# Attention masks: from identity matmuls on TensorE to the pass for the maxima on VectorE

## The reference

```python
logits = jnp.where(key_pos[None, :] <= q_pos[:, None], logits, -jnp.inf)   # layer 1
p = jax.nn.softmax(logits, axis=-1)

s = jnp.where(mask, s, NEG_INF)                                             # layer 2
m = jnp.max(s, axis=-1, keepdims=True)
e = jnp.where(mask, jnp.exp(s - m), 0.0)
```

## Time and profile before

| | us |
|---|---|
| median of 3 runs | 1828.26 (1828.24 to 1828.29) |
| span of the profiled execution | 1826.9 |
| TensorE busy | 1812.1 |
| VectorE busy | 1039.6 |
| ScalarE busy | 657.3 |
| GpSimd busy | 36.1 |

### The profile page before, as it was taken

How to read it: one execution, slowest core, us unless ns; L and a number is a source line. 1 busy time by engine, 2 the same in 40 slices (tenths; PEclk the granted TensorE clock), 3 DMA queues, 4 the chain that set the end, 5 groups by cost and what they waited for, 6 DMA issues and landing times.

```text
span 1826.9 us, 25140 instructions
## 1 busy us (share of the span) xinstructions
PE 1812.1 (99%) x9052; PEld 1510.2 (83%) x9052; DVE 1039.6 (57%) x1764; ACT 657.3 (36%) x1273; POOL 36.1 (2%) x58
## 2 busy tenths in 40 slices
PE   9999999999999999999999999999999999999998
PEld 7888888888888888878878887888888888888887
DVE  7544434434433788853358865666667666775334
ACT  6433323222223544432236343334333333343222
POOL 0000000000000000000002000000000000000001
PEclk9999999999999999999999999999999999999999
DMA  6322222222232333232238364212212222224332
GB/s 234 120 98 76 81 94 91 81 83 82 86 107 71 137 104 126 93 117 96 92 100 229 112 211 137 70 46 68 71 46 81 81 69 80 69 69 138 116 115 104
DMA packets 54179, 186.37 MB, mean 102 GB/s; under 512 B 6688, under 2 KB 7584, under 8 KB 53600
## 3 DMA queue, kind: packets, MB, share of 16 engines
q1 hardware_dynamic: 49536, 170.78, 28.2%
q0 software_dynamic: 4576, 14.68, 2.9%
HBM read 177.05 MB, written 8.39 MB: 102 GB/s over the span
## 4 chain that ended last, share of the span: by engine, by line
PE 93%; DVE 4%; DVEq 1%; ACT 1%; issue 0%; DMA 0%; SPq 0%; ACTq 0%
PE strip L430 23%; PE strip L432 23%; PE strip L431 23%; PE scores L430 3%; PE scores L431 3%; PE scores L432 3%; PE outputs L432 2%; PE outputs L431 2%; PE outputs L430 2%; PE scores L485 1%; PE scores L537 1%; PE scores L545 1%; PE scores L958 1%; PE scores L541 1%; PE scores L917 1%; PE scores L986 1%
## 5 line engine op out<-in xcount | busy, mean ns | idle before, releaser
L430 PE MATMUL strip<-xh,wh 128*128 128x512 f32 (+1 forms) x1896 | 745.7, 393 | 2.3 <-DVE xl L1968 1.3
L432 PE MATMUL strip<-xh,wl 128*128 128x512 f32 (+1 forms) x1896 | 735.5, 388 | 0.0
L431 PE MATMUL strip<-xl,wh 128*128 128x512 f32 (+1 forms) x1896 | 735.0, 388 | 0.0
L1567 DVE TENSOR_TENSOR wl<-raw,wh 128x1024 fp32r<-128x1024 f32 (+3 forms) x306 | 354.9, 1177 | 140.9 <-ACT wh L1074 140.1
L430 PEld LDWEIGHTS strip<-xh,wh 128*128 128x128 f32 x1896 | 356.3, 188 | 74.9 <-DVE xl L1968 2.6
L432 PEld LDWEIGHTS strip<-xh,wl 128*128 128x128 f32 x1896 | 356.0, 188 | 74.0
L431 PEld LDWEIGHTS strip<-xl,wh 128*128 128x128 f32 x1896 | 356.5, 188 | 69.9 <-issue 0.5
L1074 ACT ACTIVATE wh<-raw 128x1024 fp32r<-128x1024 f32 (+3 forms) x308 | 307.1, 1022 | 126.6 <-PE strip L432 87.3
L1096 ACT ACTIVATE prob<-scores,nms 128x128 f32<-128x128 f32 (+3 forms) x128 | 66.0, 533 | 131.4 <-DVE nms L1615 131.4
L1351 ACT ACTIVATE e_t<-o 128x512 f32 (+1 forms) x29 | 18.3, 632 | 213.1 <-DVE o L2048 109.2
L1575 DVE TENSOR_TENSOR y<-strip,rb 128x512 f32<-128x512 f32 x47 | 32.5, 692 | 98.8 <-PE strip L432 96.5
(11 more groups left out here) (452 smaller groups left out, 2127.1 us busy)
## 6 DMA issues: line engine op xcount, KB each, us to landing
raw<-in_w SPq DMA_DIRECT2D x308, 512.0 KB, 3.5
xn<-o POOLq DMA_DIRECT2D x4, 1024.0 KB, 7.8
xr<-xn POOLq DMA_DIRECT2D x16, 256.0 KB, 3.0
o<-in_xt SPq DMA_DIRECT2D x7, 512.0 KB, 8.5
out<-oh SPq DMA_DIRECT2D x14, 256.0 KB, 2.5
o<-in_xt POOLq DMA_DIRECT2D x13, 256.0 KB, 6.4
raw<-in_w SPq DMA_DIRECT2D x2, 256.0 KB, 3.8
o<-in_xt SPq DMA_DIRECT2D x2, 256.0 KB, 4.4
```

The lines of the kernel that those rows point to most:

```text
L430: pe.matmul(out, ah, bh, start=first, stop=False, skip_group_check=shared)
L431: pe.matmul(out, ah, bl, start=False, stop=False, skip_group_check=shared)
L432: return pe.matmul(out, al, bh, start=False, stop=last, skip_group_check=shared)
L1567: v_.tensor_tensor(wl[s][:, :cols], raw[s][:, :cols], wh[s][:, :cols].bitcast(F32), ALU.subtract)\
```

## The change

TensorE no longer adds masks. The last score matmul of a tile raises `s_done` itself, so tiles are released one by one. VectorE's pass for the maximum becomes a `tensor_tensor_reduce`: it reads the scores from PSUM and a bf16 mask from SBUF, writes the sum into `prob` (or `pc` for the compressed keys) and the row's maximum into `nm`. Before each tile, behind the wait, stands a memset of one unused column. ScalarE's exponentials read and write `prob` in place. The sign of the maxima, negated by the reduction before, moves into the scaling. The masks are stored whole: `mrow` (128 x 512, a causal block behind zeros) and `mwin` (128 x 256) replace the identity and two blocks. VectorE waits once for the constants, before the first `token_rms`. In B the maxima go by pairs of tiles, both heads in turn.

```diff
+LEAST = -3e38
...
-    identb = place("identb", [P, P], BF16)
-    maskd = place("maskd", [P, P], BF16)
-    maskw = place("maskw", [P, P], BF16)
+    mrow = place("mrow", [P, S], BF16)
+    mwin = place("mwin", [P, 2 * P], BF16)
...
-    def causal(pe, t, a):
-
-        pe.matmul(sb[t][:, P * t:P * t + P], identb[:, :], maskd[:, :], start=False, stop=True).then_inc(s_done, 1)
-
-    def pe_scores(pe, a, terms, forget=False, stacked=None, masks=NQ):
+    def pe_scores(pe, a, qq, kk, forget=False, stacked=None):
...
             if forget:
-                pe.matmul(out, selr[:, :], cum[:, keys], start=False, stop=False)
-            if t % masks == masks - 1:
-                for done in range(t + 1 - masks, t + 1):
-                    causal(pe, done, a)
+                ins = pe.matmul(out, selr[:, :], cum[:, keys], start=False, stop=True)
+            ins.then_inc(s_done, 1)
...
                 three(pe, sb[t][:, 0:w], q2[0][:, mine], q2[1][:, mine], kv["ksx"][0][:, keys], kv["ksx"][1][:, keys],
-                      True, False, True)
+                      True, True).then_inc(s_done, 1)
...
-                if t % 2:
-                    for done in (t - 1, t):
-                        out = sb[done] if PRE[done] else px
-                        ins = pe.matmul(out[:, 0:32], identb[:, :], maskc[:, 32 * done:32 * done + 32], start=False,
-                                        stop=True, skip_group_check=True)
-                        if PRE[done] == 0:
-                            ins.then_inc(sc_done, 1)
-                        c0 = PRE[done] + P * done
-                        pe.matmul(sb[done][:, c0:c0 + P], identb[:, :], maskd[:, :], start=False, stop=True,
-                                  skip_group_check=True).then_inc(s_done, 1)
...
-            a.activation(prob[:, ROW[t]:ROW[t] + w], sb[t][:, pre[t]:pre[t] + w], ACT.Exp, bias=nms[:, t:t + 1], scale=scale,
+            a.activation(prob[:, ROW[t]:ROW[t] + w], prob[:, ROW[t]:ROW[t] + w], ACT.Exp, bias=nms[:, t:t + 1], scale=scale,
                          accum_out=lsum[:, t:t + 1]).then_inc(p_exp, 1)
...
+    def masked_max(v_, out, scored, mask, most):
+
+        v_.tensor_tensor_reduce(out, scored, mask, 1.0, LEAST, ALU.add, ALU.max, most)
+
     def maxima(v_, i, scale):
 
         v_.drain()
         for t in range(NQ):
             v_.wait_ge(s_done, 4 * i + t + 1)
-            v_.tensor_reduce(nm[:, t:t + 1], sb[t][:, 0:P * (t + 1)], AX.X, ALU.max, negate=True)
+            v_.memset(nm[:, 8 + t:9 + t], 0.0)
+            masked_max(v_, prob[:, ROW[t]:ROW[t] + P * (t + 1)], sb[t][:, 0:P * (t + 1)], mrow[:, S - P * (t + 1):S], nm[:, t:t + 1])
         v_.drain()
-        v_.tensor_scalar(nms[:, 0:4], nm[:, 0:4], scale, None, ALU.mult).then_inc(nm_done, 1)
+        v_.tensor_scalar(nms[:, 0:4], nm[:, 0:4], -scale, None, ALU.mult).then_inc(nm_done, 1)
...
+        v_.wait_ge(consts_in, 16 * 5)
         token_rms(v_, 0)
...
+                v_.memset(nm[:, 8 + t:9 + t], 0.0)
+                masked_max(v_, prob[:, ROW[t]:ROW[t] + P * (t + 1)], sb[t][:, PRE[t]:PRE[t] + P * (t + 1)],
+                           mrow[:, S - P * (t + 1):S], nm[:, t:t + 1])
                 if PRE[t] == 0:
                     v_.wait_ge(sc_done, h + 1)
-                v_.tensor_reduce(nm[:, t:t + 1], sb[t][:, PRE[t]:PRE[t] + P * (t + 1)], AX.X, ALU.max, negate=True)
-                v_.tensor_reduce(nm[:, 4 + t:5 + t], (sb[t] if PRE[t] else px)[:, 0:32], AX.X, ALU.max, negate=True)
...
+                    v_.memset(nm[:, 12:13], 0.0)
+                masked_max(v_, pc[:, t, :], (sb[t] if PRE[t] else px)[:, 0:32], maskc[:, 32 * t:32 * t + 32], nm[:, 4 + t:5 + t])
...
+            for t0 in (0, 2):
+                for hh in range(2):
+                    v_.wait_ge(s_done, 4 * 32 + 8 * p + 2 * t0 + 3 + hh)
+                    v_.memset(nm[:, 8 + t0 + hh:9 + t0 + hh], 0.0)
+                    for t in (t0, t0 + 1):
+                        w = P if t == 0 else 2 * P
+                        c0 = WROW[t] - (384 if t >= 2 else 0)
+                        masked_max(v_, prob[:, BANDED * hh + WROW[t]:BANDED * hh + WROW[t] + w],
+                                   sb[2 * hh + t // 2][:, c0:c0 + w], mwin[:, 2 * P - w:2 * P],
+                                   nm[:, 4 * hh + t:4 * hh + t + 1])
```

More of the change, by code:

```diff
@@ L349, in _ @@
             if i == 5:
-                for dst, name in ((ident, "ident"), (ones, "ones"), (identb, "identb"), (maskd, "maskd"),
-                                  (maskw, "maskw"), (maskc, "maskc")):
+                for dst, name in ((ident, "ident"), (ones, "ones"), (mrow, "mrow"), (mwin, "mwin"), (maskc, "maskc")):
                     sp.dma_start(dst[:, :], d[name]).then_inc(consts_in, 16)
@@ L452, in half @@
              ready=ready, free=free if h == 0 else None)
-    def scores(pe, a, terms, last_a=None):
+    def pe_scores(pe, a, qq, kk, forget=False, stacked=None):
+        plain = stacked is None and not forget
         for t in range(NQ):
@@ L459, in scores @@
             out = sb[t][:, keys]
-            for qq, kk in terms:
-                three(pe, out, qq[0][:, mine], qq[1][:, mine], kk[0][:, keys], kk[1][:, keys], True, False)
-            yield t, out, mine, keys
-    def causal(pe, t, a):
-        pe.matmul(sb[t][:, P * t:P * t + P], identb[:, :], maskd[:, :], start=False, stop=True).then_inc(s_done, 1)
-    def pe_scores(pe, a, terms, forget=False, stacked=None, masks=NQ):
-        for t, out, mine, keys in scores(pe, a, terms):
+            ins = three(pe, out, qq[0][:, mine], qq[1][:, mine], kk[0][:, keys], kk[1][:, keys], True, plain)
             if stacked is not None:
                 pe.matmul(out, stacked[:, mine], kr[0][:, keys], start=False, stop=False)
-                pe.matmul(out, stacked[:, mine], kr[1][:, keys], start=False, stop=False)
+                ins = pe.matmul(out, stacked[:, mine], kr[1][:, keys], start=False, stop=True)
             if forget:
-                pe.matmul(out, selr[:, :], cum[:, keys], start=False, stop=False)
-            if t % masks == masks - 1:
-                for done in range(t + 1 - masks, t + 1):
-                    causal(pe, done, a)
+                ins = pe.matmul(out, selr[:, :], cum[:, keys], start=False, stop=True)
+            ins.then_inc(s_done, 1)
     def pe_turn(pe, a):
@@ L571, in pe_four @@
                 if j == KT - 1 and s == summed[1]:
-                    pe.wait_ge(consts_in, 16 * 6)
+                    pe.wait_ge(consts_in, 16 * 5)
                     pe_sum(pe, summed[0])
@@ L689, in fox @@
                     pe.wait_ge(vg_lo, 4 if h < 4 else 8)
-                    pe_scores(pe, h, [(q, k)], forget=True)
+                    pe_scores(pe, h, q, k, forget=True)
                 if s == 2:
@@ L741, in pe_mla_scores @@
         def pe_mla_scores(a, qq, kk, part):
-            pe_scores(pe, a, [(qq, kk)], stacked=qr[part])
+            pe_scores(pe, a, qq, kk, stacked=qr[part])
         def mla(p, u, n_, steps):
@@ L928, in a_head @@
             pe.matmul(po[:, :], vcp[:, g_, :], ptc[:, :], start=False, stop=False)
-            pe_scores(pe, a + 1, [(q2, kv["kw"])], masks=2)
+            pe_scores(pe, a + 1, q2, kv["kw"])
             half(pe, u.on(2), n_.base + 1, 0, n_(0))
@@ L957, in b_scores @@
                         r = slice(64 * hh, 64 * hh + 64)
[L958 to L969, removed]
+                        ins = pe.matmul(sb[2 * hh + t // 2][:, c0:c0 + w], q2[qi][r, mine], kbb[ki][r, keys],
+                                        start=t % 2 == 0 and i == 0, stop=i == 2, skip_group_check=True)
+                        if i == 2:
+                            ins.then_inc(s_done, 1)
         def b_pair(p, u, n_, steps):
@@ L2263, in a_head @@
                 v_.wait_ge(s_done, 4 * i + t + 1)
+                v_.memset(nm[:, 8 + t:9 + t], 0.0)
+                masked_max(v_, prob[:, ROW[t]:ROW[t] + P * (t + 1)], sb[t][:, PRE[t]:PRE[t] + P * (t + 1)],
+                           mrow[:, S - P * (t + 1):S], nm[:, t:t + 1])
                 if PRE[t] == 0:
                     v_.wait_ge(sc_done, h + 1)
[L2266 to L2267 removed]
+                    v_.memset(nm[:, 12:13], 0.0)
+                masked_max(v_, pc[:, t, :], (sb[t] if PRE[t] else px)[:, 0:32], maskc[:, 32 * t:32 * t + 32], nm[:, 4 + t:5 + t])
             v_.drain()
[L2269 to L2270 removed]
+            v_.tensor_scalar(nms[:, 4:8], nm[:, 4:8], -SC_A, 1e20, ALU.mult, ALU.min).then_inc(pc_exp, 1)
+            v_.tensor_scalar(nms[:, 0:4], nm[:, 0:4], -SC_A, None, ALU.mult).then_inc(nm_done, 1)
             lo(v_, u.on(2))
@@ L2340, in b_pair @@
                     x_rest(j, o[:, j, :], None, 4 * KT - 6)
[L2341 to L2348, removed]
+            for t0 in (0, 2):
[8 more added lines that the diff above has]
+                                   nm[:, 4 * hh + t:4 * hh + t + 1])
             v_.drain()
             for hh in range(2):
```

(7 more changed lines are left out.)

13 lines of the change are left out of this document (6 added, 7 removed).

## The result

The changed kernel takes 1812.89 us (median of 4 runs, 1812.62 to 1813.30) against 1828.28 for the kernel before beside it: ratio 0.991, 95% interval 0.990 to 0.993. Its profiled span is 1811.0 (before 1826.9), its clock 0.999.

The account below looks back on a forecast made before the run. TensorE, busy 99% of the span, was taken as the bound, with VectorE holding it at places around the softmax. Fox -2.4, MLA -0.5, A -2.0 and -3.3, B +1.1, start 0 summed to -7.1: 1821.2 us, range 1814 to 1833.

Parts of the forecast that it names:

- r: VectorE's price for writing out each pass's maximum by a second instruction: 0.075 us, bounds 0 to 0.17.
- m: VectorE's price for each one-column memset: 0.03 us, between 0 and 0.08.
- B: Eight B pairs: VectorE and exponentials grow 1.09 us, slack 0.99 is used up; +0.15 for six pairs, sum +1.1.
- the forecast's own rule: In B pairs, added VectorE and ScalarE time first uses up the slack before the turn; the remainder lengthens the pair.
- A: Eight A heads: first halves 0.25 us earlier each (-2.0), second halves 0.41 each (-3.3).
- e: ScalarE's extra price per exponential read from SBUF: 0.046 us, bounds 0 to 0.08; 4e = 0.18 in A's second halves.
- Fox: Eight Fox heads: VectorE no longer waits for masks, so the full 0.3 us a head is gained, -2.4.
- MLA: Eight MLA heads: five gain 0.3 us each, the first and last pair lose 0.4, 0.4 and 0.2; sum -0.5.
- Start: Kernel start: five constant loads instead of six and 96 KB more, landed in time; 0, at most 0.5 us.
- first rival: Nearly free passes, r and m near 0: about -16 us, 1812; chance 0.10.
- rival of unhidden reads: VectorE's accumulator reads don't overlap, r = 0.17: +6 us, 1834; chance 0.22.
- one price decides the sign: Price r on VectorE's passes: 0.01 us more on each costs 1.4 us of kernel; no change at r = 0.126.

Follow-up runs that it names:

- experiment 1: Changed kernel with plain reductions and exponentials from PSUM as before the change, and no masks added anywhere: 1807.63 us, ratio 0.988.
- experiment 5: Changed kernel with ScalarE taking exponentials from the unchanged scores in PSUM, all masks zero: 1810.46 us, ratio 0.990.
- experiments 7 and 8: Changed kernel with eight more 32-column passes in each B pair, as plain reductions (1818.45 us), then as masked passes with accumulator output (1820.07 us).
- experiment 9: Changed kernel with two more one-column memsets ahead of each maximum pass of the B pairs: 1814.89 us, ratio 0.992.
- experiment 4: Kernel before the change, each tile's mask matmul right behind its scores, so tiles are released one by one: 1827.24 us, ratio 0.9992.

## Why the prediction was wrong

The runs take the change apart, in us (each part good to about 0.5):

| step | median | part |
|---|---|---|
| before | 1828.6 | |
| mask matmuls gone | 1813.9 | -14.6 |
| tiles released one by one | 1807.6 | -6.3 |
| masked passes, reads, memsets | 1810.5 | +2.8 |
| exponentials from SBUF | 1812.9 | +2.4 |

**The step that failed is the price r of "writing the maximum out".** I took 0.075, the distance of two of VectorE's smallest instructions, from a row in which they follow each other alone. The read does exist, but it runs beside the next pass: 0.013 each. I had even seen the case, ScalarE's accumulator reads, 210 ns long and overlapped, and priced by the worse row. With m (0.03 taken, 0.008 found) it is one error: the queue of a B pair grew by 0.14, not 0.72; that of A's first half, where 0.75 was forecast, by 0.16 from the first pass to the scaled maxima (2.31 against 2.15 in experiment 1), and its division comes 0.28 to 0.38 later, counted from the turn before. The forecast had also called the lower bound of r, 0, out of reach, since the pass would be two instructions. The second instruction is there, but it cost 0.013, close to that bound.

- **B** (+1.1 forecast, -3.0 measured). The working was right and its sizes wrong. With the measured prices the pair grows by 0.14 + 0.30 = 0.44 against a slack of 0.94, so the forecast's own rule gives -0.50 a pair in the loop; -0.43 was measured. TensorE's masks were 0.76, not 0.86. The last pair got longer by 0.51, not by 1.09.
- **A** (-5.3 forecast, -9.5 with what lies between the layers). By the starts of the turns the second halves gained 0.56 to 0.76, 0.68 on average (forecast 0.41), the first halves 0.50 on average (forecast 0.25). The starts alone mislead. In the first half the turn takes each tile when VectorE has divided it, so VectorE holds it to its end. The ten transposes of the second A head before the change, after it, and in experiment 1:

```profile
1176.73 1.64 PE L917 MATMUL scores<-ident,prob 128*128 128x128 f32 x10
```

```profile
1171.47 1.61 PE L895 MATMUL scores<-ident,prob 128*128 128x128 f32 x10
```

```profile
1171.04 1.26 PE L895 MATMUL scores<-ident,prob 128*128 128x128 f32 x10
```

  Counted from the end of one turn (the first matmul behind its ten transposes) to the end of the next, the first halves gained 0.53 to 0.78 and the second 0.51 to 0.58. Two readings of the forecast fail besides r. In the second halves TensorE sets the pace itself, in the changed kernel and in experiment 5 alike, so 4e = 0.18 is not paid there (0.04 is). In the first halves the masks were said to hold VectorE 0.12 at the start; it still sits idle 0.23 before its first pass (0.20 before the change, and 0.20 in experiment 1 without any mask), so those 0.12 were never to be had.
- **Fox** (-2.4, measured -2.2) came as forecast: 0.28 a head, the slack ahead of the turn growing from 3.00 to 3.63.
- **MLA** (-0.5, measured -0.8): four of the five middle heads gained 0.27 to 0.37, the fifth 0.05; the first and the two last lost 0.06, 0.12 and 0.33, where 0.4, 0.4 and 0.2 were forecast. In the last pair TensorE now waits for the output strips' `xl` (2.4 us in three waits of the kernel, before 1.3), a late piece that I had not named.
- **e**: 0.046 taken, 0.037 measured. It bites in B, as I said, with 2.1 of the 2.4 us; in A's second halves, where I had put 1.4, it is 0.3.
- **Start**: the first Fox turn came 0.66 us earlier, 0.28 of which is that head's; in two profiled runs of one kernel it differs by up to 0.3, between the kernels here, whose start is the same, by up to 1.1, so I count the rest as scatter.

So the first rival, nearly free passes, is what happened, with its time (1812) and nearly its places (B gained 0.43 a pair in the loop where it had 0.57); it had a chance of 0.10 only. The rival of unhidden reads is excluded by experiments 7 and 8. That "one price decides the sign" was right: at 1.4 us per 0.01, the 0.062 too much for r are 8.7 us, about the 8.3 missed. That the two agree so well is in part luck: the forecast's 1.4 us for e in A's second halves and its 1.0 us for an earlier start in the first ones were wrong in opposite directions. A price that carries so much deserved wider chances on its low side, since the nearest row of the same kind already showed overlap.

## What to carry to other kernels

An operation's second row is not its price: look where the next instruction starts. A maximum taken on the way through VectorE cost 0.013 us over the plain reduction, so a mask added there is nearly free even where VectorE is on the path, as long as the result goes to SBUF: 2.8 us here for 224 passes, most of it where VectorE holds TensorE. And a matmul that is taken away gives more than its own time if it also held back a semaphore: here the release by single tiles was worth 6 us, against 14.6 for the matmuls. And where a consumer takes tiles one by one, the start of its work says little: look at its end. Where VectorE then sets the pace, look in its queue for work that fits into its next wait.

## What the runs showed of the hardware

- Which memory a pass writes shows in the accumulator's read behind it: 83 ns behind a pass into SBUF, 145 behind one into PSUM, the maximum going to SBUF in both. The Trainium skill (Perfetto Trace Analysis, section Optimizing Scalar/DVE Operations) gives VectorE's overhead per instruction as about 60 ns on SBUF and 125 on PSUM, ScalarE's as about 93 and 51. The differences, 65 and 42, are close to the 62 seen here and to ScalarE's 0.037 us for an exponential read from SBUF. Whether it is the same overhead that shows in the read, no run tells.
- A one-column memset starts beside a pass (59 ns long, 0.008 us of spacing in experiment 9). The 0.08 between two scalings in the earlier trace rows was no price for it.
- A mask of 128 columns by itself costs TensorE 0.13 us: in experiment 4 the last Fox scores and the second strip matmul stand 101.74 - 101.15 = 0.59 apart, with no mask between them 101.40 - 100.94 = 0.46.

```profile
101.15 0.40 PE L475 MATMUL scores<-cum,selr 128*128 128x512 f32 x1
101.39 0.23 PE L466 MATMUL scores<-maskd,identb 128*128 128x128 bf16 x1
101.43 0.48 PE L430 MATMUL strip<-xh,wh 128*128 128x512 f32 x1
101.74 0.40 PE L431 MATMUL strip<-xl,wh 128*128 128x512 f32 x1
```

```profile
100.94 0.40 PE L465 MATMUL scores<-cum,selr 128*128 128x512 f32 x1
101.17 0.39 PE L429 MATMUL strip<-xh,wh 128*128 128x512 f32 x1
101.40 0.40 PE L430 MATMUL strip<-xl,wh 128*128 128x512 f32 x1
```
